# A reordered mixer, tail and merge in a single-core fp32 decoder layer

## The chip, the core and the metric

The kernel runs on one core of a Trainium2 chip: TensorE (PE) multiplies, VectorE (DVE), ScalarE (ACT) and GpSimd (POOL) do the elementwise work, SyncE (SP) and ScalarE issue transfers. The metric is the device time of one launch in microseconds; less is better.

## The reference

One layer of a hybrid decoder runs over 1024 prompt tokens and 8 × 8 sample tokens, width 1024, all in float32:

```python
x = x + 0.5 * swiglu(rmsnorm(x, g_ffn1), w1_gate, w1_up, w1_down)      # d_ff 2816
z = rmsnorm(x, g_mix) @ w_in       # mLSTM q,k,v,i,f,o | attention q,k,v (3 groups) | 2 gates
y_m = mlstm_scan(...) -> per-head rmsnorm, o-gate, @ w_up_m             # 4 heads, dk = dv = 128
y_a = dilated attention, (window, dilation) = (128,1), (512,4), (2048,16); groups combined
      by softmax denominators, @ w_up_a                                 # 4 heads of 64 a group
x = x + (sigmoid(gm) * y_m + sigmoid(ga) * y_a) @ w_out
x = x + 0.5 * swiglu(rmsnorm(x, g_ffn2), w2_gate, w2_up, w2_down)
y = rmsnorm(x, g_final)            # and the new states and caches
```

The sample tokens attend to cached keys and values of past tokens, eight sequences of eight tokens.

## The kernel before

Tokens stand in the free dimension, 1088 of them, in four quarters of 272. Each weight and each activation is split into a high part (rounded for the fast matmul format) and a low part; a product is three matmuls: high·high, high·low, low·high. Weights come in 99 slabs of 2048 columns by SyncE.

**Half steps.** The gate and up products use a scheme with seven products in place of eight (`WINO`, L85), a block of the weight slab and of the tokens each. For each, `fast` (L1036) waits for the low weight piece (`wcl_done`), for the token piece (`xprep`) and for free banks (`wino_step`, nine steps of VectorE a unit in `gate_part`). A unit is one slab and half of the tokens. GpSimd makes the low pieces (`low`, L843) and the sums of weight blocks (`less`, L850) of a slab in `gate_split`; ScalarE makes the high pieces: `PLAIN` ones from the slab itself, `SUMS` and `LAST` ones from the sums (L1522). Token pieces are made by `prepare` (VectorE, L2089 and L2095) and `token_high` (ScalarE, L1513). The first units of both half steps are written out one by one; a loop (two units per slab) follows. A unit of gates ends with a hidden row set stored by SyncE, and the down products read these rows back: `load_hidden` on the queue of `x_reload`, 22 times, with `accumulate` (L2132) adding into the residual.

**Mixer.** Queries, keys, values and gates are projected, then a program of 36 steps `w` (four heads, nine chunks) runs mLSTM chunk work, with one prompt attention unit of 35 (`UNITS`) beside each, `LEAD` = 3 units ahead. `att_exps`, `att_copy` run on ScalarE, `att_max`, `att_out` (L2471, L2472) on VectorE; SyncE stores each unit's rows (`store_outputs`) to `o_att`. The SP queue also loads caches and states in this stretch, in an order written out by hand.

**Tail.** After the steps come the last states, the last head's norm and turn (`turn_head`), then the sample attention in two quads of four sequences (`s_scores`, `s_max`, `s_exps`, `s_turn`, `s_values`, `s_out_turn`), with four groups of prompt rows loaded from `o_att` (`load_groups`), weighted and summed (`combine`, L2575 to L2592), transposed (`c_turn`, L1394) and stored (`store_pair`). GpSimd splits the three slabs of the up projection.

**Merge and out projection.** 32 units (quarter × eighth of the width) multiply the six branch pieces by the up slabs in two bank pairs; VectorE applies the gates from `sgate` (L2639, L2641, L2643), ScalarE makes the high part (L1954) and VectorE the low part (L2645) ahead of the next unit. `branch_high` and `branch_low` (L1912, L2607) split the next quarter's six branch pieces. GpSimd splits the first out-projection slab after the last unit (L829, L834). Then the out projection runs, with the norms and first slab of the second half step beside its end.

## Time and profile before

| | us |
|---|---|
| median of 3 runs | 2762.98 (2760.33 to 2774.57) |
| the profiled execution | 2771.38 |
| its span | 2769.5 |
| TensorE busy in it | 2514.5 |

One stretch follows another: start of the first half step to 112, its loop to 536, down products to about 840, projections to 1443, attention units ahead and mixer steps to 1657, tail to 1745.5, merge to 1850.5, a gap to 1861, out projection to 1960, start of the second half step to 2059.5, its loop to 2466, down products to 2740, last norm. To read the profile: a timeline row gives the start, the length and, in brackets, how long the engine sat idle before and what ended this; TensorE's granted clock is given as a share of its upper level of 2.4 GHz.

### The profile page before, as it was taken

The page shows a single profiled execution, that of the slowest core. Times are in us where ns is not written, and L with a number is a line of the kernel's source. Part 1 is how long each engine was busy: PE and PEld are TensorE (multiplying, and loading weights), DVE is VectorE, ACT ScalarE, POOL GpSimd, SP SyncE. Part 2 cuts the span into 40 slices and gives each one's busy share as a digit, 9 for nine tenths or more (in the row PEclk, how much of TensorE's full clock was granted, in tenths as well). Part 3 has the DMA queues.
Part 4 walks back from the last instruction along what each step waited for, and adds up shares of the span by engine and source line. Part 5 has one row for each costly group of instructions (what it writes and reads, how often), then busy time and mean ns, then how long its engine had stood idle before and what let it go on. Part 6 is the DMA issues. An engine that isn't in the chain of part 4 may idle for free. (4 is left out here: it accounts for less than half of the span.)

```text
span 2769.5 us, 47348 instructions
## 1 busy us (share of the span) xinstructions
PE 2514.5 (91%) x17550; PEld 2452.1 (89%) x17550; DVE 1261.0 (46%) x2482; ACT 593.7 (21%) x1165; POOL 1348.7 (49%) x1945
## 2 busy tenths in 40 slices
PE   4899999899999999999988885579789999989996
PEld 3899999899989999999986672579789999989996
DVE  6444434466684101332005555543653334446667
ACT  4322233110131011000114431111422323211012
POOL 5577777464445343444402313023557777746430
PEclk9899999999999999999997897789889999999998
DMA  2111221342213322222215737441112211143201
GB/s 113 70 70 74 78 81 70 144 164 94 78 35 127 127 96 92 88 93 98 78 53 173 231 122 287 159 137 64 67 51 74 89 70 74 70 189 131 94 16 65
DMA packets 112121, 282.89 MB, mean 102 GB/s; under 512 B 12996, under 2 KB 65404, under 8 KB 97020
## 3 DMA queue, kind: packets, MB, share of 16 engines
q1 hardware_dynamic: 87368, 251.65, 25.8%
q10 hardware_dynamic: 24628, 29.50, 3.0%
q8 instruction: 88, 1.44, 0.2%
q14 instruction: 37, 0.30, 0.0%
HBM read 206.25 MB, written 74.85 MB: 102 GB/s over the span
## 5 line engine op out<-in xcount | busy, mean ns | idle before, releaser
L1054 PE MATMUL ps<-chi,wch 128*128 128x272 f32 x2464 | 718.9, 292 | 50.7 <-POOL wcl L843 34.0
L1056 PE MATMUL ps<-chi,wcl 128*128 128x272 f32 x2464 | 717.5, 291 | 0.0
L829 POOL TENSOR_TENSOR wsp<-raw,con 128x256 fp32r<-128x256 f32 x440 | 269.8, 648 | 772.2 <-PE ps L979 284.8
L843 POOL TENSOR_TENSOR wcl<-raw,wch 128x256 fp32r<-128x256 f32 x616 | 450.7, 764 | 350.1 <-ACT wch L1522 350.1
L1054 PEld LDWEIGHTS ps<-chi,wch 128*128 128x128 f32 x2464 | 471.2, 191 | 53.7 <-POOL wcl L843 36.0
L1056 PEld LDWEIGHTS ps<-chi,wcl 128*128 128x128 f32 x2464 | 470.4, 191 | 0.0
L1055 PE MATMUL ps<-xlo,wch 128*128 128x272 f32 x1408 | 411.1, 292 | 0.0
L979 PE MATMUL ps<-act_hi,wsp 128*128 128x384 f32 (+1 forms) x1056 | 353.2, 334 | 23.6 <-DVE x L2132 14.8
L982 PE MATMUL ps<-act_lo,wsp 128*128 128x384 f32 (+1 forms) x1056 | 350.0, 331 | 0.0
L983 PE MATMUL ps<-act_hi,wsp 128*128 128x384 f32 (+1 forms) x1056 | 349.7, 331 | 0.0
L2132 DVE SCALAR_TENSOR_TENSOR x<-ps,x 128x384 f32<-128x384 f32 (+1 forms) x528 | 276.0, 532 | 161.7 <-PE ps L983 144.9
L834 POOL TENSOR_TENSOR wsp<-raw,wsp 128x256 fp32r<-128x256 f32 x440 | 326.1, 776 | 0.0
L1006 PE MATMUL ps<-h_hi,wsp 128*128 128x384 f32 (+1 forms) x960 | 314.6, 328 | 2.9 <-issue 1.8
L1010 PE MATMUL ps<-h_hi,wsp 128*128 128x384 f32 (+1 forms) x960 | 314.2, 327 | 0.0
L1009 PE MATMUL ps<-h_lo,wsp 128*128 128x384 f32 (+1 forms) x960 | 314.1, 327 | 0.0
L1055 PE MATMUL ps<-clo,wch 128*128 128x272 f32 x1056 | 304.8, 289 | 0.0
L1055 PEld LDWEIGHTS ps<-xlo,wch 128*128 128x128 f32 x1408 | 272.4, 193 | 0.0
L850 POOL TENSOR_TENSOR raw<-raw 128x256 f32<-128x256 f32 x352 | 261.8, 776 | 0.0
L1522 ACT ACTIVATE wch<-raw 128x512 fp32r<-128x512 f32 x308 | 182.8, 625 | 237.3 <-POOL raw L850 237.3
L979 PEld LDWEIGHTS ps<-act_hi,wsp 128*128 128x128 f32 x1056 | 201.8, 191 | 27.1 <-DVE x L2132 16.8
L982 PEld LDWEIGHTS ps<-act_lo,wsp 128*128 128x128 f32 x1056 | 201.9, 191 | 0.9 <-issue 0.6
L983 PEld LDWEIGHTS ps<-act_hi,wsp 128*128 128x128 f32 x1056 | 201.9, 191 | 0.0
(263 smaller groups left out, 3956.3 us busy)
## 6 DMA issues: line engine op xcount, KB each, us to landing
raw<-stream SPq DMA_DIRECT2D x99, 1024.0 KB, 4.8
hidden_out<-gout SPq DMA_DIRECT2D x88, 272.0 KB, 2.0
hst<-hidden_out SPq DMA_DIRECT2D x22, 1088.0 KB, 5.1
vc<-vc_in SPq DMA_DIRECT2D x8, 1170.0 KB, 7.8
kc<-kc_in SPq DMA_DIRECT2D x8, 1152.0 KB, 9.1
sgate<-zgate SPq DMA_DIRECT2D x32, 272.0 KB, 2.9
x<-xT SPq DMA_DIRECT2D x3, 2176.0 KB, 8.4
zgate<-stage ACTq DMA_DIRECT2D x16, 384.0 KB, 2.5
```

The costliest lines, as they stand in the source:

```text
L834: low_part = pool.tensor_tensor(wlo[j][:, cut], raw[:, j, cut], whi[j][:, cut].bitcast(F32), ALU.subtract)
L843: ins = pool.tensor_tensor(wcl[b][p][:, cut], raw[:, b, col + a:col + a + SPLIT], wch[b][p][:, cut].bitcast(F32), ALU.subtract)
L979: mm = pe.matmul(out, w_hi, x_hi, start=(k == 0), stop=False)
L982: pe.matmul(out, w_hi, x_lo, start=False, stop=False)
L983: last = pe.matmul(out, w_lo, x_hi, start=False, stop=(k == nk - 1))
L1006: mm = pe.matmul(out, w_hi, h_hi[:, k, a:a + w], start=(k == 0), stop=False)
L1009: pe.matmul(out, w_hi, h_lo[:, k, a:a + w], start=False, stop=False)
L1010: mm = pe.matmul(out, w_lo, h_hi[:, k, a:a + w], start=False, stop=(k == KT - 1))
L1054: pe.matmul(out, wch[b][p][:, cut], chi[q][p][:, k, :], start=(k == 0), stop=False)
L1055: pe.matmul(out, wch[b][p][:, cut], lo[:, k, :], start=False, stop=False)
L1056: mm = pe.matmul(out, wcl[b][p][:, cut], chi[q][p][:, k, :], start=False, stop=(k == 3))
L2132: dve.scalar_tensor_tensor(x[:, d, a:a + w], bank(4 + v % 4, w), 0.5, x[:, d, a:a + w], ALU.mult, ALU.add).then_inc(acc_free, 1)
```

## The change

- The order of the seven products, and with it that of the low pieces, the high pieces, the token pieces and the gate's steps, is another: the first two need plain pieces only. ScalarE's copy of a unit's first product waits for all nine steps of the unit before (it waited for seven). ScalarE makes sums and last pieces of the first slabs earlier. `load_hidden` goes ahead of `x_reload`, and VectorE waits for the second half of the reloaded residual only at the second group.
- Six attention units run ahead (`LEAD`), with head 0's first work at the fourth; stores go by ScalarE's queue.
- Quad 0 of the sample attention runs inside steps 29 to 35: query copies, scores, maxima, exponentials and turns; group 0 is combined there. Quad 1's values come inside the merge. Caches, group 0 and up slabs are asked for in the steps, each group's load and store by ScalarE's queue; ScalarE makes the up slabs' high parts.
- The merge has three bank pairs instead of two, and the low part of a unit comes one unit later; the kept residual is loaded at unit 16 instead of unit 2; the first out-projection slab is split in the last quarter into a place of its own (`out_hi`, `out_lo`).

The core of the diff:

```diff
-WINO = ((0, 9, 1), (1, 16, 6), (2, 17, 4), (3, 18, 5), (0, 14, 3), (1, 19, 2), (2, 10, 7))
+WINO = ((0, 9, 1), (1, 10, 2), (2, 16, 5), (3, 17, 4), (0, 18, 6), (1, 19, 3), (2, 11, 7))
...
+def next_branches(c, d):
+
+    if c == 0:
+        return (2 * d - 10, 2 * d - 9) if d >= 5 else ()
+    return (d - 2,) if d >= 2 else ()
+
+
+def out_bank(v):
+
+    return 4 + (v - AU_OUT + 2) % 4
...
-LEAD = 3
+LEAD = 6
+HEAD_AT = 3
+W_QUERY, W_SCORE, W_MAX, W_TURN, W_TURNED = 29, 31, 32, 33, 34
...
+                load_hidden(n, 0)
                 x_reload(n, 0)
-                load_hidden(n, 0)
...
+            def load_third():
+
+                sp.wait_ge(o_ready, last_of[0] + 1)
+                load_keys(2)
+                load_values(2)
...
+            for load in behind:
+                load()
...
                     else:
+                        sp.wait_ge(o_ready, last_of[1] + 1)
                         load_new(sqs, qr)
+                        for j in range(4):
+                            sp.dma_start(smk[SROW * j:SROW * j + SROW, :], amasks[0:SROW, A_SAMP:A_N]).then_inc(s_const, 16)
+                        load_new(sks, kr_out)
                         for b in (1, 2):
                             load_values_s(b)
...
+                if w + LEAD == last_of[0]:
+                    load_third()
...
+                    if h == H - 1:
+                        for s in range(2):
+                            sp.wait_ge(o_stored[s], 16 * len(UNITS[s::2]))
+                        sp.wait_ge(sqb_ready, 1)
+                        for n in range(2):
+                            sp.dma_start(oc[:, n], o_att[n * P:(n + 1) * P]).then_inc(c_in, 16)
+                        for i in range(3):
+                            slab(S_UP + i, (S_UP + i) % 3)
...
+                        load_vnw()
                         load_values_s(3)
...
+                        sp.wait_ge(sample_scored, 1)
+                        for b in range(4, 8):
+                            load_keys_s(b)
...
+            sp.wait_ge(sv_full, 1)
+            for b in (5, 6, 7):
+                load_values_s(b)
...
             sp.wait_ge(sample_scored, 2)
-            for i in (1, 2):
-                slab_behind(S_UP + i, (S_UP + i) % 3)
-            store_pair(1)
+            load_values_s(4)
...
+                    if c + 1 < NP:
+                        for k in next_branches(c, d):
+                            if k == 4 and c < 2:
+                                sp.wait_ge(mix_stored, 16 * (c + 3))
+                            load_branch(c + 1, k)
+                    if n == 10:
+                        sp.wait_ge(soT_ready, QUADS)
+                        for h in range(H):
+                            sp.dma_start(mix[4 + h // 2, 64 * (h % 2):64 * (h % 2) + 64, SEQ:TOK],
+                                         soT[:, h].rearrange("d b t -> d (b t)")).then_inc(hidden_stored, 16)
+                        sp.wait_ge(hidden_stored, 16 * 2 * H)
...
+                    if n == 16:
+
+                        sp.wait_ge(mix_stored, 16 * PAIRS)
                         sp.dma_start(x[:, 0:XB], x_kept[:, 0:XB]).then_inc(x_in[1], 16)
...
                 low(0, 0, 1)
-                low(5, 1536, 2)
-                low(4, 512, 3)
+                low(1, 512, 2)
+                low(5, 1536, 3)
                 less(0, 1024, 0)
                 less(1024, 1536, 1024)
                 pool.wait_ge(wsum_done, 4 * s + 1)
                 less(1536, 1536, 0)
-                low(2, 0, 4)
-                low(3, 1024, 5)
-                low(1, 1536, 6)
+                low(3, 0, 4)
+                low(2, 1536, 6)
+                low(4, 1024, 5)
                 pool.wait_ge(wsum_done, 4 * s + 3)
                 less(512, 512, 1536)
                 low(6, 512, 7)
...
+            for s in range(S_UP, S_UP + 3):
+                j = s % 3
+                for n, a in enumerate(range(0, SLAB, SPLIT)):
+                    cut = slice(a, a + SPLIT)
+                    pool.wait_ge(hi_split, s * PIECES + n + 1 - PIECES)
+                    low_part = pool.tensor_tensor(wlo[j][:, cut], raw[:, j, cut], whi[j][:, cut].bitcast(F32), ALU.subtract)
...
+            pool.wait_ge(up_full, PU_UP + 3 * KT)
+            pool.wait_ge(mx_ready, 6 * NP)
+            split(S_OUT, S_OUT // 3, S_OUT % 3, out_hi, out_lo)
...
-                    if p == 0 and not (isinstance(u, int) and u < 2):
-                        pe.wait_ge(wino_step, 9 * u - 10)
+                    if p < 3 and not (isinstance(u, int) and u < 2):
+                        pe.wait_ge(wino_step, 9 * u - (13, 12, 10)[p])
...
                 att_turn(u)
                 att_scores(u + 1)
-                if u == 0:
+                if u == HEAD_AT:
...
+                if w == W_SCORE:
+                    s_scores(0)
+                if w == W_TURN:
+                    s_turn(0)
             last_states()
+            s_values(0)
             for c in range(NC):
                 turn_head(H - 1, c)
...
+            s_out_turn(0)
             c_turn(0)
-            s_turn(0)
             s_scores(1)
-            s_values(0)
             c_turn(1)
             s_turn(1)
-            s_out_turn(0)
             c_turn(2)
-            s_values(1)
-            s_out_turn(1)
             c_turn(3)
...
+                    par = (KT * c + d) % 3
+                    pe.wait_ge(pair_free, unit)
...
+                    if (c, d) == (0, 1):
+                        s_values(1)
+                    if (c, d) == (0, 4):
+                        s_out_turn(1)
...
-            PLAIN = ((0, 0, 0), (5, 1536, 0), (4, 512, 0))
-            SUMS = ((2, 0, 1), (3, 1024, 2), (1, 1536, 3))
+            PLAIN = ((0, 0, 0), (1, 512, 0), (5, 1536, 0))
+            SUMS = ((3, 0, 1), (4, 1024, 2), (2, 1536, 3))
...
                 if half == 0:
                     act.wait_ge(wino_full, 7 * u + 1)
                     if not (isinstance(u, int) and u == 0):
-                        act.wait_ge(wino_step, 9 * u - 2)
+                        act.wait_ge(wino_step, 9 * u)
                     act.activation(gsil[:, 0, :], bank(4 * par, QW), ACT.Copy).then_inc(gate_silu, 1)
                 elif half == 1:
-                    act.wait_ge(wino_step, 9 * u + 5)
-                    act.activation(gsil[:, 0, :], gsil[:, 0, :], ACT.Silu).then_inc(gate_silu, 1)
+                    act.wait_ge(wino_step, 9 * u + 1)
+                    act.activation(gsil[:, 1, :], gsil[:, 1, :], ACT.Silu).then_inc(gate_silu, 1)
                 else:
                     act.wait_ge(wino_step, 9 * u + 8)
-                    act.activation(gsil[:, 1, :], gsil[:, 1, :], ACT.Silu).then_inc(gate_silu, 1)
+                    act.activation(gsil[:, 0, :], gsil[:, 0, :], ACT.Silu).then_inc(gate_silu, 1)
...
-                    token_high(0, 0)
                     act.wait_ge(x_in[2], 16)
                     half_square(1, 0)
                     half_square(1, 1)
+                    first_slab(0, SUMS)
+                    half_square(1, 2)
+                    half_square(1, 3)
+                    half_square(1, 4)
+                    token_high(0, 0)
                     token_high(0, 1)
                     token_high(0, 2)
-                    half_square(1, 2)
-                    half_square(1, 3)
+                    first_slab(0, LAST)
+                    gate_high(X + 1, b1, loaded + 16, PLAIN)
+                    half_square(1, 5)
                     token_high(0, 3)
                     token_high(0, 4)
...
+                    gate_silus(U, 0, 0)
+                    half_root(f1)
+                else:
+                    half_root(f1)
+                    gate_silus(U, 0, 0)
+                    first_slab(n, LAST)
+                    gate_high(X + 1, b1, loaded + 16, PLAIN)
+                gate_high(X + 1, b1, loaded + 16, SUMS)
                 gate_silus(U, 0, 1)
-                token_high(f1, 0)
-                gate_high(X + 1, b1, loaded + 16, SUMS)
+                gate_high(X + 1, b1, loaded + 16, LAST)
                 gate_silus(U, 0, 2)
                 gate_silus(U + 1, 1, 0)
+                gate_silus(U + 1, 1, 1)
+                token_high(f1, 0)
...
+            def store_outputs(u):
+
+                g, blk, h0, nh, nk = UNITS[u]
+                act.wait_ge(o_ready, u + 1)
+                o = o_att[:, g, h0:h0 + nh, :]
...
+            def up_high(s):
+
+                j = s % 3
+                act.wait_ge(raw_in[j], 16 * (s // 3) + (16 if j else 0))
+                act.wait_ge(slab_free, s + 1)
+                act.wait_ge(sample_scored, 2)
+                act.wait_ge(sv_full, 1)
+                for a in range(0, SLAB, SLAB // 2):
+                    cut = slice(a, a + SLAB // 2)
+                    act.activation(whi[j][:, cut], raw[:, j, cut], ACT.Copy).then_inc(hi_split, PIECES // 2)
...
-                if u == 0:
+                if u > 0:
+                    store_outputs(u - 1)
+                if u == HEAD_AT:
...
+                if u <= NU:
+                    store_outputs(u - 1)
...
+                if w == W_MAX:
+                    s_exps(0)
+                if w == W_TURN:
+                    group_exps(0)
+                if w == W_TURNED:
+                    s_turned(0)
             head_squares(H - 1)
+            next_group(1)
             head_roots(H - 1)
-
...
-            s_exps(0)
+            store_pair(0)
             group_exps(1)
-            s_turned(0)
+            next_group(2)
             s_exps(1)
+            for i in range(3):
+                up_high(S_UP + i)
+            store_pair(1)
+            s_turned(1)
+            group_exps(2)
+            next_group(3)
+            store_pair(2)
             for k in range(4):
                 branch_high(0, k)
-            s_turned(1)
-            group_exps(2)
             group_exps(3)
+            store_pair(3)
             for k in (4, 5):
                 branch_high(0, k)
...
-                if c == 3 and r == 3:
+                if c == 3 and r == 1:
                     act.wait_ge(slab_ready, S_OUT + 4)
                     first_slab(1, PLAIN)
-                if c == 3 and r == 5:
+                if c == 3 and r == 4:
                     first_slab(1, SUMS)
...
-                if m == 6:
-                    dve.wait_ge(wino_step, 9 * u + 6)
-                if m == 7:
-                    dve.wait_ge(wino_step, 9 * u + 4)
+                if m in (6, 7, 8):
+                    dve.wait_ge(wino_step, 9 * u + (6, 5, 4)[m - 6])
                 if m in (6, 8):
                     dve.wait_ge(gate_silu, 3 * u + m // 2 - 1)
-                out, one, two = ((S, B, G1), (U4, C, S), (gup[:], E, U4), (S, E, S), (G1, A, G1),
-                                 (Y1, B, U4), (Y1, G1, Y1), (G2, C, S), (Y2, G2, gup[:]))[m]
+                out, one, two = ((G2, B, G1), (S, C, G1), (U4, E, S), (gup[:], A, U4), (S, A, S),
+                                 (Y1, B, U4), (Y1, G2, Y1), (G1, C, S), (Y2, G1, gup[:]))[m]
                 dve.tensor_tensor(out, one, two, ALU.mult if m in (6, 8) else ALU.add).then_inc(wino_step, 1)
...
-                def downs(i, j):
+                def downs(i, j, first=False):
                     for c in range(NC):
+                        if first and c == 1:
+                            dve.wait_ge(x_in[2], 32 * (n + 1))
                         for d in range(KT):
...
             for u in range(LEAD):
                 att_out(u)
                 if u + 2 <= LEAD:
                     att_max(u + 2)
+                if u == HEAD_AT - 1:
+                    args(0)
+                    sample_arg(0)
+                    dve.memset(qwb[:], 0.0)
+                    link(dve.memset(ssq[:], 1.0))
...
+                if w == W_QUERY:
                     sample_queries()
+                if w == W_MAX:
+                    s_max(0)
+                if w == W_TURN:
+                    group_max(0)
+                if w == W_TURNED:
+                    s_turned(0)
+                    group_weigh(0)
+                if w == 9 * H - 1:
+                    group_sum(0)
             for part, o in (((0, 1, 2), (3, 0)), ((3, 4, 5), (2, 0)), ((6, 7), (3, 0))):
                 sample_states(H - 1, part, o)
             head_sums(H - 1)
+            s_outputs(0)
...
+            s_out(0)
             c_out(0)
-            s_turned(0)
             combine(1)
             s_max(1)
-            s_outputs(0)
+            c_out(1)
+            s_turned(1)
+            combine(2)
+            c_out(2)
...
             combine(3)
             c_out(3)
             for k in (4, 5):
                 branch_low(0, k)
...
+                    if n > 0:
+                        merge_low(n - 1)
+                    if (c, d) == (0, 2):
+                        s_outputs(1)
+                    if (c, d) == (0, 4):
+                        s_out(1)
+                    if c + 1 < NP:
+                        for k in next_branches(c, d):
+                            branch_low(c + 1, k)
+            merge_low(KT * NP - 1)
```

## Rows read from the trace of the kernel before

**Rows 1.** The page, parts 1 (busy) and 6 (KB each, us to landing).

```profile
PE 2514.5 (91%) x17550; PEld 2452.1 (89%) x17550; DVE 1261.0 (46%) x2482; ACT 593.7 (21%) x1165; POOL 1348.7 (49%) x1945
...
hst<-hidden_out SPq DMA_DIRECT2D x22, 1088.0 KB, 5.1
```

**Rows 2.** By stretch: length, engines' busy time, granted clock, DMA share, GB/s.

```profile
0.00:112.00 112.00, 63.21 (x384) 57.80 (x384) 71.83 (x84) 45.34 (x67) 53.58 (x65) 0.89 0.24 89
...
1474.00:1657.00 183.00, 157.17 (x1052) 132.13 (x1053) 110.96 (x357) 78.93 (x192) 48.12 (x93) 0.86 0.52 168
1657.00:1745.50 88.50, 37.30 (x439) 21.90 (x438) 52.13 (x91) 11.31 (x24) 33.63 (x48) 0.71 0.62 228
1745.50:1850.50 105.00, 84.24 (x576) 82.32 (x576) 58.77 (x144) 18.05 (x49) 0.00 (x0) 0.88 0.54 169
```

**Rows 3.** TensorE's waits, whole span: releaser, total us, times, longest.

```profile
PE ps L1054 <- POOL wcl L843: 34.0, 5, 10.7
PE ps L1394 <- DVE yat L2592: 30.1, 3, 16.0
...
PE ps L1054 <- DVE xlo L2095: 12.5, 3, 6.9
...
PE ps L979 <- POOL wsp L834: 10.6, 2, 10.4
...
PE ps L1287 <- DVE ao L2472: 6.2, 2, 4.5
```

**Rows 4.** Timeline of TensorE, first half step (start, us, instruction, idle before).

```profile
67.91 0.60 PE L1054 MATMUL ps<-chi,wch 128*128 128x272 f32 x1 [10.66 <-POOL wcl L843]
```

**Rows 5.** Groups on GpSimd in the first 115 us (count, busy, mean ns).

```profile
L843 POOL TENSOR_TENSOR wcl<-raw,wch 128x256 fp32r<-128x256 f32 x41 | 35.9, 906 | 58.9 <-ACT wch L1522 58.9
```

**Rows 6.** Timeline of TensorE where the first half step turns to down products.

```profile
540.79 0.55 PE L979 MATMUL ps<-act_hi,wsp 128*128 128x384 f32 x1 [4.45 <-DVE act_lo L2138]
...
551.46 0.69 PE L979 MATMUL ps<-act_hi,wsp 128*128 128x384 f32 x1 [4.66 <-DVE x L2132]
```

**Rows 7.** Timeline of the SP queue there.

```profile
528.45 0.71 SPq L522 DMA_DIRECT2D hst<-hidden_out  x1
```

**Rows 8.** Timeline of VectorE and GpSimd, a slab within the loop.

```profile
183.13 4.42 POOL L850 TENSOR_TENSOR raw<-raw 128x256 f32<-128x256 f32 x6
...
186.05 0.91 DVE L2118 TENSOR_TENSOR gout<-gsil,gout 128x272 f32<-128x272 f32 x1
```

**Rows 9.** The same at the loop's end, and TensorE's wait behind it.

```profile
499.27 4.22 POOL L850 TENSOR_TENSOR raw<-raw 128x256 f32<-128x256 f32 x6
...
502.24 7.08 DVE L2118 TENSOR_TENSOR gout<-gsil,gout 128x272 f32<-128x272 f32 x1
...
510.48 0.39 PE L1054 MATMUL ps<-chi,wch 128*128 128x272 f32 x1 [1.40 <-ACT gsil L1541]
```

**Rows 10.** Timeline of TensorE in the mixer: attention values, mLSTM scores.

```profile
1466.95 1.97 PE L1287 MATMUL ps<-av,apt 128*128 128x65 f32 x8
...
1484.69 0.28 PE L1166 MATMUL ps<-con,kT 128*128 128x128 f32 x1
...
1488.02 0.28 PE L1166 MATMUL ps<-con,kT 128*128 128x128 f32 x1
```

**Rows 11.** Waits in the mixer (engine, line, releaser: total us, times, longest).

```profile
DVE ao L2471 <- DMA o_att<-ao: 20.1, 4, 8.1
```

**Rows 12.** Timeline of TensorE in the tail.

```profile
1742.72 1.12 PE L1394 MATMUL ps<-con,yat 128*128 128x128 f32 x4 [13.65 <-DVE yat L2592]
```

**Rows 13.** Timeline of VectorE in the tail.

```profile
1729.31 8.32 DVE L2575 TENSOR_TENSOR ocm<-oc 128x8 f32<-128x8 f32 x1
```

**Rows 14.** Groups in the tail, both quads, all four groups.

```profile
L1374 PE MATMUL ps<-vc,spt 128*32 128x260 f32 x144 | 12.4, 520 | 2.1 <-issue 2.1
```

**Rows 15.** Groups in the merge.

```profile
L979 PE MATMUL ps<-mx_hi,wsp 128*128 128x272 f32 x192 | 61.0, 318 | 22.3 <-DVE mh_lo L2645 11.9 <-DVE mx_lo L2607 10.4
```

**Rows 16.** Timeline of TensorE, start of the second half step.

```profile
1993.56 0.60 PE L1054 MATMUL ps<-chi,wch 128*128 128x272 f32 x1 [10.32 <-POOL wcl L843]
```

595 lines of the change are left out of this document (269 added, 326 removed).

## The prediction

> **What bounds the kernel now.** I read the page's first part, the same figures by stretch, the waits of TensorE, and then the timeline of each stretch where it waits. TensorE is busy for 2514.5 of 2769.5 us [rows 1], so about 255 us are idle, and nothing that leaves TensorE's work as it is can gain more than that, apart from the clock. The change takes no matmul of the large products away. By stretch [rows 2]: the start of the first half step idles 112.0 - 63.2 = 48.8 us, the mixer's steps 183.0 - 157.2 = 25.8, the tail 88.5 - 37.3 = 51.2, the merge 105.0 - 84.2 = 20.8. The out projection's first split adds 10.6 at most [rows 3], and the second half step starts with waits, one of 10.3 [rows 16]. The loops between these stretches keep TensorE full; there the change matters only by the second rival.
>
> The sums below are made against the profiled execution, 2771.4 us (its span of 2769.5 and 1.9 around it). The median of the runs shown is 2763.0, 8.4 less.
>
> **A. First units of the first half step.** The new product order asks for plain weight pieces in its first two products, where the old one asked in its second for the sixth low piece, which GpSimd makes after the sums. That wait was 10.66 us [rows 4]. Over the whole span, waits for low weight pieces (34.0 in 5) and for the token sums' low part (12.5 in 3) are 46.5 us [rows 3], nearly all of it at the two starts; here they are 10.7 + 4.9 + 3.4 = 18.9 us on the path, so 27.6 at the second. Not all of it goes: GpSimd makes the same pieces, 41 low pieces took 35.9 us, 0.91 each [rows 5], and those of the last products still have to come. I let eight pieces by 0.91 = 7.3 us return as waits of later products, and take 18.9 - 7.3, rounded to 11. Ends: all three short waits kept and two thirds of the long one gone, 6; nearly all gone, 15. The new order of ScalarE's copies adds no instruction; the cover is its idle time (45.3 busy of 112 [rows 2]).
>
> **B. Turn from gate to down products, first half step.** TensorE waits 4.45 and again 4.66 us [rows 6]. The hidden rows are asked for at 528.45 [rows 7], 0.6 behind a residual reload on the same queue; the change swaps the two and lets VectorE wait for the last part of the residual only ahead of the second group. The load of the hidden rows then runs first on its queue, and lands, by the 5.1 us that such a load takes in the median [rows 1], before the gates end at 536. Both waits go: 9.1 us, and the down products' first matmuls run a little earlier at a higher granted clock; I take 9.5, ends 7 (half of the second wait comes back, for the residual comes later now) and 10.5. **G. The same turn in the second half step** has the same two waits, so 9.5 again, ends 7 and 13 because it starts from the lower granted clock there.
>
> **C and D. Mixer and tail.** Six attention units instead of three run ahead of the mLSTM steps, so the first step starts later: a unit took 4.4 us at the lower clock (the values at 1466.95 [rows 10] began 4.4 after those of the unit before), three more cost 13 to 17. In return the last three attention units leave the steps: with attention a step takes 3.33 us (two score matmuls at 1484.69 and 1488.02 [rows 10]), and three steps without it are cheaper by about 2 each, 6 to 7 together. VectorE's waits for stored attention rows, 20.1 us in four [rows 11], come from stores that stand on the SP queue behind cache loads; the stores now go by ScalarE's queue and should not wait for these loads. TensorE shares only part of that wait; I take 14 back, between 10 and 18. A wait of 4.5 us early in the steps, where VectorE stood behind GpSimd [rows 3], goes too. Inside the last seven steps the sample attention of quad 0 is added: its query copies, scores, row maxima, exponentials and transposes. In the tail the same work took about 15 us of TensorE and VectorE time one after the other, so the steps get 14 to 17 longer. Sum: 15 - 6.5 - 14 - 4.5 + 15 = +5, the steps end at 1662 instead of 1657.
>
> The DMA issues move as well: 35 attention stores go from SP to ScalarE, 29 of them in the steps, at 0.4 to 0.7 us of issue each (0.71 for a larger one [rows 7]), which ScalarE has (78.9 of 183 busy [rows 2]). Behind each store wait on ScalarE's queue stand the next exponentials. The store of a unit is placed two exponentials behind its own work, so that it finds its rows written; if they are late, ScalarE stops, and TensorE with it. Bounds: nothing (a gain is excluded, the issue is only moved), and 29 by 0.4 = 12 us; I take nothing, since TensorE is what ends a step.
>
> Here the Trainium skill speaks against the move, "DMA: Bandwidth & Descriptors", section "Queues, rings and completion order": each DMA engine takes turns between the queue rows it has work for, by packets, so that a second queue escapes the order of the first but not its traffic. With DMA at 0.52 of its time in these steps [rows 2] I read it so that the stores go through at once but more slowly; by the rule taken alone half of the 14 us would stay, and the sum would be 7 us worse. Waits of up to 8.1 us [rows 11] look like a queue's order rather than a shared engine, so I stay with 14.
>
> The tail is the larger gain. From the end of the steps to the merge are 88.5 us, 51 of them idle on TensorE [rows 2], and 30.1 of these are waits for combined attention groups [rows 3]: the last came 13.65 us late [rows 12], behind a VectorE instruction that took 8.32 us [rows 13] while GpSimd split the up-projection weights. After the change the chain is, from the end of the steps: values of quad 0, half of 12.4 [rows 14] and the wait ahead, 11; turn of the heads to 16; group 0 combined meanwhile, its matmul at 19; group 1 at 24, one group being 5 us of small VectorE work; scores and maxima of quad 1; high parts of the up weights on ScalarE, six of about 1 us by an estimate; exponentials of quad 1 at 35; group 2, then the load of group 3, landing at about 44; group 3 and its transposes to 50; the last two branch parts stored and read back to 55. So 55 in place of 88.5, with ends 45 (group loads hidden) and 75 (each of two loads seen in full, 10 us each). Merge begins at 1662 + 55 = 1717 instead of 1745.5: gain 28.5, ends 10 and 40.
>
> **E. Merge and first out-projection split.** The merge's 84.2 busy us at a granted clock of 0.88 are 74 at full clock [rows 2]; of its idle time 22.3 us come from late low parts and quarter boundaries [rows 15]. Delaying the low part by one unit takes VectorE's part off the path, and the early split of the out weights takes off the wait of 10.4 that follows the merge [rows 3]. Added: values of quad 1 and their turn, 6.2 + 1.0 [rows 14]. New sum: 74 + 7 + three quarter boundaries of 2.6 + a clock start of 3 + 8 of DMA waits, since the residual's load of 3.3 MB and the store of sample rows still stand ahead of gate loads. That is 100 against 105.0 + 10.4 = 115.4: gain 15, ends 5 (values and one long gate wait stay on the path) and 28 (none does).
>
> **F. First units of the second half step.** The 27.6 us from above, 10.32 of them in one wait [rows 16]. The same reordering applies, and ScalarE starts the first slab one step earlier, but ScalarE's and GpSimd's work of a slab is the same, and the residual's norm still comes ahead. I take 40%, 11; ends 6 and 16.
>
> **Sum.** 11 + 9.5 + 9.5 + 28.5 + 15 + 11 = 84.5. 2771.4 - 84.5 = 2686.9 for a profiled execution, 8.4 less for the median: **2679 us**. The low ends add to 41 (2722), the high ones to 122.5 (2640).
>
> **Rivals.** First, **the tail does not shrink**: the group loads from memory and VectorE's chain set the merge's start, as they do now with waits of up to 16.0 us [rows 3], and the added work in the steps costs what the shorter tail saves. For it: one set of load buffers, now beside cache loads and up weights. Against: the first group and three up slabs are asked for inside the steps. Then C and D give 3 instead of 28.5, and E 8: 2763 - 52 = **2711**. Chance 0.12.
>
> Second, **VectorE is locked out in each slab of the loops**. At 186.05 the combination of two SBUF inputs took 0.91 us, 2.92 behind GpSimd's first subtraction at 183.13 [rows 8]; at 502.24, 2.97 behind it, it took 7.08 and ended only when GpSimd paused, and TensorE then waited 1.40 [rows 9]. The change rearranges both engines' order in a slab, and lets the next unit's ScalarE copies wait for the whole previous unit (two combinations more, about 0.6), so a blocked slab costs 1.4 + 0.6 = 2.0. If VectorE comes 0.05 us later against GpSimd in each of the 40 slabs, that is 80 us, and the gain is nearly gone: 2763 - 84.5 + 80 = **2759**. For it: the two rows are only 0.05 us apart. Against: the long form stands only three times in this trace, at the ends of the loops, and VectorE's work of a slab is not lengthened. Chance 0.08.
>
> Of this the Trainium skill says, in "SBUF — State Buffer", section "Who interferes with whom", that a VectorE instruction with two SBUF inputs and a GpSimd instruction that reads SBUF exclude each other, the first holding the shared ports for its whole instruction. The row agrees that it blocks; its 7.08 us are ten GpSimd instructions of 0.70, where the rule gives one. By the rule a meeting would cost 0.7 us, within what the loop takes without a wait, and this rival's time would be the forecast's.
>
> Third, **slower than before**: the same lock, from the same point, but in every place where the new order puts VectorE behind running GpSimd work. Besides the 80 us it then strikes the four first units, 2 us each, and the tail: the quad maxima and group combinations wait until GpSimd's 24 low parts of the up weights have ended, and the 8.32 us row [rows 13] becomes 10 more. 80 + 8 + 10 = 98 against 84.5, 2763 + 14 = **2777**. It decides from the point at which VectorE's combination comes more than 2.95 us after the first subtraction. Chance 0.06.
>
> **How the numbers follow.** Forecast 0.74, first rival 0.12, second 0.08, third 0.06. About 0.5% (14 us) is what a measurement of this kernel can tell from no change. Faster by over that: forecast and first rival, 0.86; within it: the second, 0.08 (2759); slower: 0.06. The range takes in the bounds of the sum, 2640 to 2722, and the first rival with some spread: 2643 to 2735.
>
> **What would show it.** A: the second product of the first pass follows its first without a gap. B: the hidden rows are asked for ahead of the residual, and neither of the two waits at the turn is over 1 us. C: no wait of VectorE for stored attention rows above 3 us; the steps end near 1662. D: 55 us from there to the merge's first matmul. E: no 10 us gap after the merge, 100 us for the stage. F: 11 us off the first units. In the loops the two-input combination stays at 0.9. The forecast fails where a slab of the loop shows 7 us in that row, or where the tail stays above 75 us because a group's load or a moved store is late.

## The result and the profile after

The changed kernel takes 2728.2 us in the median (2723.5 to 2732.6, four runs) against 2764.9 of the kernel before: ratio 0.986, interval 0.984 to 0.988. The forecast was 2679 in a range of 2643 to 2735: the time lies inside the range, near its slow end, and less than half of the expected 84.5 us came (37 us between the medians). The profiled execution has a span of 2727.0 us, 42.5 less than that of the kernel before, and its parts can be read stage by stage.

The page's first part, and the stretches that answer to [rows 1] and [rows 2] (start of the first half step, attention ahead with the first step, the other steps, tail, merge; columns as there):

```profile
PE 2500.2 (92%) x17548; PEld 2432.9 (89%) x17550; DVE 1249.4 (46%) x2482; ACT 599.1 (22%) x1171; POOL 1337.3 (49%) x1921
```

```profile
0.00:107.00 107.00, 63.51 (x375) 55.87 (x375) 73.28 (x83) 44.61 (x65) 54.03 (x60) 0.87 0.24 91
1434.00:1481.50 47.50, 23.02 (x122) 16.52 (x121) 15.55 (x40) 13.67 (x31) 8.51 (x17) 0.66 0.81 244
1481.50:1658.00 176.50, 148.61 (x1080) 122.40 (x1082) 108.38 (x356) 76.07 (x186) 38.72 (x77) 0.88 0.50 168
1658.00:1720.80 62.80, 28.74 (x268) 17.91 (x266) 43.11 (x80) 15.48 (x27) 20.15 (x24) 0.66 0.74 268
1720.80:1823.80 103.00, 86.75 (x664) 82.41 (x664) 58.42 (x145) 18.14 (x49) 10.22 (x16) 0.91 0.53 170
```

The last step ends only near 1664 here, so the fourth row still holds some 6 us of the steps.

TensorE's waits over the span, beside [rows 3]:

```profile
PE ps L982 <- DVE x L2195: 26.2, 8, 7.1
PE ps L1369 <- DVE yat L2614: 21.8, 2, 12.5
...
PE ps L1057 <- DVE xlo L2160: 20.0, 5, 9.5
...
PE ps L982 <- DVE mx_lo L2636: 13.2, 3, 6.4
PE ps L1291 <- DMA av<-va_out: 11.9, 1, 11.9
...
PE ps L1057 <- ACT gsil L1550: 9.6, 6, 5.6
...
PE ps L1209 <- DVE Cs L2475: 7.2, 1, 7.2
...
PE ps L982 <- DVE mh_lo L2710: 3.0, 1, 3.0
...
PE ps L1057 <- POOL wcl L836: 3.0, 3, 1.7
```

Four more rows of the same view of the kernel before:

```profile
PE ps L979 <- DVE x L2132: 15.5, 7, 4.7
...
PE ps L1166 <- DMA v<-vm: 10.6, 1, 10.6
...
PE ps L1054 <- ACT gsil L1541: 3.9, 3, 1.4
...
PE ps L1287 <- DMA av<-va_out: 2.1, 1, 2.1
```

The wait for low weight pieces, 34.0 us before, has nearly gone (3.0), and the merge's 10.6 us split too (0.2). In their place stand the token pieces (`xlo`, 20.0 against 12.5), the down accumulation (26.2 against 15.5), ScalarE's copies of the gates (`gsil`, 9.6 against 3.9) and, in the mixer, `Cs`. The wait of 11.9 us for the first attention values (`av`) is no new loss: the kernel before waited 10.6 us for `v` and 2.1 for `av` in that place.

Taking the same matmul in both timelines as a mark gives what each stage gained (us, before less after):

| stage | forecast | measured |
|---|---|---|
| A, start of the first half step | 11 | 3.2 |
| end of its loop | 0 | 1.7 |
| B, turn and down products | 9.5 | 3.6 |
| projections | 0 | 1.8 |
| C, attention ahead and steps | -5 | -16.4 |
| D, tail | 33.5 | 30.9 |
| E, merge, split, out projection | 15 | 14.0 |
| F, start of the second half step | 11 | 7.4 |
| end of its loop | 0 | 1.7 |
| G, turn and down products | 9.5 | -6.2 |
| last norm | 0 | 0.8 |
| sum | 84.5 | 42.5 |

Tail and merge came nearly as forecast, the second start with two thirds of its 11 us. Four terms did not come: A, B, C and G together are 41 us short, nearly the whole miss of 42. Each entry compares one profiled execution with another: the projections, which should not change, take 620.6 to 627.2 us in the profiles of kernels that leave GpSimd's splits as they are, so an entry can be off by a few us.

### The profile page after: what moved, and what is told of

The parts are those of the page before. It is cut to its first block and busy times, and to the rows that moved or that the text cites. A ratio compares the mean times of both kernels' runs of the same rounds, so it can differ in the third digit from the quotient of the medians.

```text
span 2727.0 us, 47602 instructions
## 1 busy us (share of the span) xinstructions
PE 2500.2 (92%) x17548; PEld 2432.9 (89%) x17550; DVE 1249.4 (46%) x2482; ACT 599.1 (22%) x1171; POOL 1337.3 (49%) x1921
## 5 line engine op out<-in xcount | busy, mean ns | idle before, releaser
L836 POOL TENSOR_TENSOR wcl<-raw,wch 128x256 fp32r<-128x256 f32 x616 | 457.6, 776 | 334.2 <-ACT wch L1531 334.2
L822 POOL TENSOR_TENSOR wsp<-raw,con 128x256 fp32r<-128x256 f32 x408 | 250.0, 648 | 602.3 <-PE ps L982 287.0
L827 POOL TENSOR_TENSOR wsp<-raw,wsp 128x256 fp32r<-128x256 f32 x408 | 301.2, 774 | 0.0
```

The costliest lines, as they stand in the source:

```text
L827: low_part = pool.tensor_tensor(lo[:, cut], raw[:, j, cut], hi[:, cut].bitcast(F32), ALU.subtract)
L836: ins = pool.tensor_tensor(wcl[b][p][:, cut], raw[:, b, col + a:col + a + SPLIT], wch[b][p][:, cut].bitcast(F32), ALU.subtract)
```

## What happened at the four places

**The turn.** After, around 531 to 552 us, SP, ScalarE, VectorE and TensorE:

```profile
533.65 0.55 SPq L528 DMA_DIRECT2D x<-xT  x1
...
535.00 0.43 SPq L535 DMA_DIRECT2D hst<-hidden_out  x1
...
548.73 0.84 ACT L1565 ACTIVATE act_hi<-hst 128x768 fp32r<-128x768 f32 x1 [14.70 <-DMA hst<-hidden_out]
549.60 1.37 DVE L2201 TENSOR_TENSOR act_lo<-hst,act_hi 128x768 fp32r<-128x768 f32 x1 [8.36 <-ACT act_hi L1565]
...
551.50 0.69 PE L982 MATMUL ps<-act_hi,wsp 128*128 128x384 f32 x1 [6.61 <-DVE x L2195]
```

The first wait of [rows 6] is gone, from 4.45 to 0.42. The second one has grown from 4.66 to 6.61 and ends at the same 551.5 us as before: VectorE stands in its order behind the low part of the next hidden rows, which land 13.7 us after they are asked for, behind the residual's second half and a weight slab on the queue.

The second turn has one more wait:

```profile
2444.82 4.61 POOL L822 TENSOR_TENSOR wsp<-raw,con 128x256 fp32r<-128x256 f32 x8
2447.59 8.11 DVE L2201 TENSOR_TENSOR act_lo<-hst,act_hi 128x768 fp32r<-128x768 f32 x1 [0.38 <-ACT act_hi L1565]
...
2449.39 5.50 POOL L827 TENSOR_TENSOR wsp<-raw,wsp 128x256 fp32r<-128x256 f32 x8
...
2456.16 0.63 PE L982 MATMUL ps<-act_hi,wsp 128*128 128x320 f32 x1 [6.03 <-DVE x L2195]
```

The low part took 8.11 us where its median is 0.96. It ends at 2455.7, 0.8 us after the GpSimd run (2454.9) whose last 16 instructions stand above. I call a VectorE row that ends only behind such a run a long row, and the effect the lock. It is the lock of the second rival, but on another instruction than I named.

**The mixer.** Waits between 1500 and 1545 us, after:

```profile
DVE Cp L2467 <- DMA c_out<-Cp: 9.8, 1, 9.8
...
PE ps L1209 <- DVE Cs L2475: 7.2, 1, 7.2
```

SP's order there:

```profile
1516.86 0.32 SPq L604 DMA_DIRECT2D aqk<-qr  x1
...
1521.16 1.60 SPq L689 DMA_DIRECT2D c_out<-Cp  x1
```

SP issued eight key loads and one value load of the third group first, from 1516.86 on, and head 0's state store only at 1521.16, behind them. VectorE waits for that store before it may overwrite the state. In the kernel before the store came first.

**The first start.** The third unit's third product is the late one now, in place of the second unit's second ([rows 4]):

```profile
86.19 0.57 PE L1057 MATMUL ps<-chi,wch 128*128 128x272 f32 x1 [9.30 <-DVE xlo L2160]
```

## The experiments

My theory after the two traces: each missing gain was returned at the next wait (A, B), the state store (C) and the lock (G). Rivals stand with the runs. Ratios are to the kernel before, with their intervals. Where a run's whole time hides a stage, the stage is read from its timeline, that is, from one execution.

**The two halves apart.** The parts of the diff for the half steps alone, and all the rest alone.

> The kernel before with the half steps' part of the change alone (product order, order of pieces and of ScalarE's copies, hidden rows ahead of the residual). Theory, the half steps' gains were given back at the next wait: read from the two traces they are 3 + 2 at the first start and the end of its loop, 4 at its turn, 7 + 2 at the second start, and a loss of 6 at the second turn, so about 11 us under the kernel before (ratio 0.996). Had my four terms held, 41 us (0.985). Rival, the two halves of the change disturb one another: then this kernel alone comes near 41.

> The kernel before with mixer, tail, merge and first out-projection split of the change alone. Theory: 14 us from mixer and tail and 14 from merge and out projection, together 28 under the kernel before (ratio 0.990). By my terms it would be 43.5 (0.984). If the halves disturb one another, this gives clearly more than 28, and the two kernels' gains do not add to that of the whole change.

Half steps alone: 0.997 (0.994 to 0.9998). The rest alone: 0.992 (0.990 to 0.995), 21 us. The halves add up to 29 against 39 of the whole change, with intervals that touch; no gain of the size I had forecast is hidden in either. The half steps gave 8 us of 41: the largest part of the miss is there.

**The swap undone.**

```diff
-                load_hidden(n, 0)
                 x_reload(n, 0)
+                load_hidden(n, 0)
...
+                dve.wait_ge(x_in[2], 32 * (n + 1))
-                downs(0, (S_D[n] + 1) % 3, True)
+                downs(0, (S_D[n] + 1) % 3)
```

> The changed kernel with the residual's reload again ahead of the hidden rows, and VectorE's wait for the whole residual again ahead of the first group, in both half steps. My terms B and G say that this costs 19 us against the changed kernel. Theory, the turn is set by the transfers that can start only after the last gates, so that what the first wait gives the second takes: at most 5 us are lost in the first half step, the second TensorE wait falls from 6.6 to 4 or 5 there, and in the second half step the 8.1 us row of VectorE's activation low part may go, so between 4 us faster and 6 us slower than the changed kernel.

0.988 (0.983 to 0.994): by the ratios 7 us slower than the changed kernel, with intervals that overlap. TensorE's first wait is back (4.72 us at the first turn, 5.91 at the second), and its second is 4.93 and 4.36. From the start of the last gate matmul to the end of the last down product it took 288.4 and 282.8 us, the changed kernel 282.0 and 289.6, the kernel before 285.7 and 283.4. So the swap saved no 19 us. The first figure includes a low part of 4.63 us; the second has none, and there the swapped order without a long row, below, takes 278. The swap is worth some 5 us there, where I wrote 9.5.

**The third group's loads later.**

```diff
-                if w + LEAD == last_of[0]:
+                if w + LEAD == last_of[0] + 2:
                     load_third()
```

> The changed kernel with the loads of the third group's keys and values issued two steps later, so that head 0's state store stands ahead of them on the SP queue. Theory: VectorE's 9.8 us wait for that store, and TensorE's wait of 7.2 us behind it, go, 4 to 8 us faster than the changed kernel. Rival, the transfer engines are full in this stretch whatever the order: the wait moves to the next load, and the time stays within 2 us.

0.982 (0.979 to 0.985), 11 us less than the changed kernel by the ratios, 8 between the medians. The store is issued ahead of the loads, and both waits shown for the mixer are gone:

```profile
1514.04 0.34 SPq L689 DMA_DIRECT2D c_out<-Cp  x1
```

The steps 1 to 12 take 48.2 us where the changed kernel took 59.2 and the kernel before 56.0; over all profiles with six units ahead they take 48.2 to 48.7 with the later loads and 58.9 to 61.4 without. The whole of stage C takes 209.5 us in place of 224.5 (208.0 in the kernel before). So the cause of C's loss is shown. This run also had no long row at the second turn, 278.0 us. Its gain over the changed kernel has therefore two causes.

**The low part one group later**, from here on with the third group's loads later.

```diff
-                        hidden_low(i + 1, c, j)
+                        if not first:
+                            hidden_low(i + 1, c, j)
+                        elif c > 0:
+                            hidden_low(i + 1, c - 1, j)
+                    if first:
+                        hidden_low(i + 1, NC - 1, j)
```

> The kernel with the third group's loads two steps later, and in the first round of down products VectorE's low part of the next hidden rows one group later in its order. Theory: TensorE's second wait at the turn (6.6 us in the first half step, 7.1 in the second) is VectorE standing behind the next hidden rows, which are loaded behind the residual's second half and a weight slab; the down products do not need that low part yet. Then the second wait falls to 2 us or less and each turn gains 4 to 5. Rival: VectorE stands behind the residual's second half itself; the waits stay within 1 us of 6.6, no gain.

0.976 (0.973 to 0.980). TensorE's second wait is 0.65 us at the first turn and 0.71 at the second, in place of 6.6 and 5.4 with the later loads alone. The stretch takes 279.9 us at the first, in spite of a low part of 5.12 us later in it, and 271.7 at the second, 6.4 less. TensorE's next wait at the first turn, then VectorE's rows at the place of the old one:

```profile
564.77 0.44 PE L982 MATMUL ps<-act_hi,wsp 128*128 128x384 f32 x1 [0.65 <-DVE x L2195]
```

```profile
548.64 0.56 DVE L2195 SCALAR_TENSOR_TENSOR x<-ps,x 128x384 f32<-128x384 f32 x1 [0.50 <-PE ps L986]
551.15 1.49 DVE L2195 SCALAR_TENSOR_TENSOR x<-ps,x 128x384 f32<-128x384 f32 x3 [1.95 <-DMA x<-xT]
```

The residual is 1.95 us late here, and TensorE does not feel it. The second wait was VectorE's order, not the residual.

**Pauses in GpSimd's splits.**

```diff
+                    if n:
+                        pool.wait_ge(low_split, s * (PIECES - 1) + n - (PIECES - 1))
                     low_part = pool.tensor_tensor(lo[:, cut], ...)
+                    if n + 1 < PIECES:
+                        low_part.then_inc(low_split, 1)
```

(and the same with `hi_split` for the high parts.)

> The kernel with the third group's loads two steps later, and each GpSimd instruction of a slab's split waiting for the one before it to end. Theory of the lock: a VectorE instruction with two SBUF inputs that meets running GpSimd work gets in only when GpSimd pauses; with a pause after each instruction no low part of hidden rows takes over 2 us beside a split, where it took 8.11 us once in the changed kernel and 4.63 to 8.35 in two other runs. The gate's combination beside the other GpSimd routine is left as it is and may still show 7 us. Time within 3 us of the kernel with later loads, 6 us less where that one had a long row in the down products. Rival: what frees VectorE is the end of GpSimd's work, and the long rows stay.

> The changed kernel with each GpSimd instruction of a slab's split waiting for the one before it to end, and nothing else. Theory: the 8.11 us row of VectorE's activation low part in the second half step goes, and with it some 10 us of the second turn and its down products (289.6 us from the last gate to the last down product in the changed kernel, 278 to 280 here). The whole is 5 to 10 us faster than the changed kernel. Rival: the second turn's loss is the transfers', and it stays above 285 us.

Whole times: 0.977 (0.975 to 0.980) on top of the later loads, by the ratios 13 us less than with these alone, which is more than I had expected and not explained; and 0.984 (0.981 to 0.988) on the changed kernel alone, a median of 2728.4 us against 2728.2, by the ratios 5 us less and well inside the intervals. The lock is gone from the low parts of hidden rows: in the four profiles with paused splits none of 264 takes over 1.6 us, in the ten others 30 of 660 take over 2. Changed kernel, then the changed kernel with pauses (count; shortest, median and longest in ns):

```profile
L2201 DVE TENSOR_TENSOR act_lo<-hst,act_hi x66: 818/959/8110, 530.9 to 2676.8; 128x768 fp32r<-128x768 f32 x44, 128x640 fp32r<-128x640 f32 x22
```

```profile
L2210 DVE TENSOR_TENSOR act_lo<-hst,act_hi x66: 818/958/1541, 532.3 to 2674.5; 128x768 fp32r<-128x768 f32 x44, 128x640 fp32r<-128x640 f32 x22
```

The second turn takes 277.9 us in place of 289.6, as the theory said; the later loads without a pause also had 278.0 there, so the count of long rows is the stronger evidence. The 5 to 10 us for the whole are neither shown nor excluded. The profiled execution lost 4.4 us in the projections and had two 7 us rows in the gate loops, where nothing was changed (2.6 and 2.4 us of delay).

**Four units ahead.** `LEAD` 4 and `HEAD_AT` 1 in place of 6 and 3.

> The kernel with the third group's loads two steps later, and four attention units ahead of the steps in place of six. In the traces a unit ahead costs 4.0 to 4.4 us (lower clock, one unit after the other), a unit inside a step 1.6 to 2. Theory: the first step starts 8 to 9 us earlier, the steps are 3 to 4 us longer, so 4 to 6 us faster. My term C (13 to 17 us for three units, 6.5 back) says 5 us. Rival: the units in steps 29 and 30 meet the sample attention there and the gain is lost by the end of the steps.

0.983 (0.978 to 0.988), no gain in the whole, for this profile holds two long low parts (9.07 and 8.12 us) and turns of 292.1 and 288.7. In the mixer, from the first attention matmul to the second step's scores 36.2 us in place of 47.5, and from there to the last step 168.3 in place of 161.9: 4.9 us gained, within the expected 4 to 6, though each side was mis-sized by 2 to 3.

**The second half's reciprocal earlier.** `half_root` of the second half ahead of the first unit's copy, `half_inverse` ahead of its combinations.

> The kernel with the third group's loads two steps later, and the reciprocal of the second half's norm, first half step, made on VectorE ahead of the first unit's combinations instead of behind five of them. Theory: what replaced the waits for low weight pieces at the first start is the chain of token pieces on VectorE, so moving 3.5 us of it ahead takes 3 to 4 us off the 9.3 us wait of TensorE at the third unit, and the loop starts 3 to 4 us earlier. Rival: the third unit is held by GpSimd's or ScalarE's pieces, and the wait stays.

0.981 (0.978 to 0.985). The loop starts 3.7 us earlier (sixth unit), as expected. The 9.3 us row itself stays, because the products ahead of it moved as well:

```profile
82.84 0.57 PE L1057 MATMUL ps<-chi,wch 128*128 128x272 f32 x1 [9.08 <-DVE xlo L2160]
```

The token chain of VectorE sets the first start. The whole shows no gain over the later loads: a low part of 8.41 us stands in the first turn (292.1 us).

**Together.** All five edits in one, then with pauses in the gate slabs' routine too.

> Third group's loads two steps later, low part of the next hidden rows one group later in the first down round, reciprocal of the second half's norm ahead of the first combinations, four attention units ahead in place of six, pauses in the splits. If the parts add: against the kernel with later loads alone, 4 to 5 and 6 at the two turns, 4 at the start, 5 in the mixer: 18 to 20 us less, 2690 to 2705, ratio to the kernel before 0.973 to 0.976. Rival: what one part gives the next wait takes, and it is no faster than the best of them alone (0.976 to 0.977).

> The same with pauses between GpSimd's instructions in the gate slabs' routine too. Theory of the lock: no two-input combination of the gates takes over 2 us in the loops any more, which saves 2 to 8 us (two to four rows of 7 us in each profile, each with 1.4 to 4 us of TensorE behind it). Rival: the pauses lengthen a slab's 16 us of GpSimd to about 18, and the first units, which wait for it, lose 2 to 4 us each.

All five: 2702.1 us, 0.974 (0.972 to 0.977), the fastest median of the study and within what was expected, though its interval overlaps that of the later low part (0.973 to 0.980), so the rival is not excluded. At the turns TensorE now waits 4.2 and 3.7 us for GpSimd's paused splits (279.3 and 274.9 us), and the projections took 633.1 us against 625.0 to 625.4 in the other three profiles with paused splits, which no run explains. All six: 0.978 (0.976 to 0.981), 10 us more than all five between the medians. The two-input combination of the gates in the two, all five first:

```profile
L2190 DVE TENSOR_TENSOR gout<-gsil,gout x88: 435/510/7232, 60.4 to 2406.0; 128x272 f32<-128x272 f32 x88
```

```profile
L2213 DVE TENSOR_TENSOR gout<-gsil,gout x88: 441/713/999, 60.0 to 2412.4; 128x272 f32<-128x272 f32 x88
```

No gate row is over 1 us any more. But from the fifth to the seventh unit the first start takes 29.5 us in place of 24.6 and the second 28.0 in place of 24.7: the rival's price, 3 to 5 us each, is more than the long rows had cost (in all five a wait of 1.7 us behind each of two).

**The changed kernel again.**

> The changed kernel once more, nothing altered. If the long rows of the lock depend on where VectorE and GpSimd happen to stand (their distance differs by hundredths of a microsecond between a row of 0.9 and one of 7), this profile has them at other places than the first one: no 8 us row at the second turn, that turn at 278 to 280 us from the last gate to the last down product in place of 289.6, and perhaps another row elsewhere. If they are fixed by the program's order, the row of 8.1 us and the 289.6 us come again within 1 us.

0.985 (0.978 to 0.991), its profile 17.1 us longer than the first one. The parts differ like this: a gate row of 7.45 us at 139.8 delays the first loop by 4.2 us, a low part of 8.59 us the first turn by 10.2 (292.2), the projections take 4.2 us more, and the second turn (a low part of 8.77, the turn's fifth, as in the first profile) takes 286.4 instead of 289.6. The low part of the first turn, and GpSimd's run beside it:

```profile
562.35 8.59 DVE L2201 TENSOR_TENSOR act_lo<-hst,act_hi 128x768 fp32r<-128x768 f32 x1 [0.38 <-ACT act_hi L1565]
```

```profile
560.04 4.63 POOL L822 TENSOR_TENSOR wsp<-raw,con 128x256 fp32r<-128x256 f32 x8
564.62 5.51 POOL L827 TENSOR_TENSOR wsp<-raw,wsp 128x256 fp32r<-128x256 f32 x8
```

So the program does not fix how often the lock strikes. The place at a turn it does: all seven low parts over 8 us in the profiles are the fifth of their turn, and a long row came again at the second turn. The expectation that it comes again within 1 us falls, and so does the one that it does not come. Over all profiles with the swapped order and VectorE's old order, a turn without a low part over 8 us takes 282.0 to 282.7 us at the first and 277.5 to 278.7 at the second, one with such a row 292.1 to 292.2, and 286.4 to 289.6. Such a row in the down products costs 8 to 12 us.

Most meetings of the two engines pass. In the first profile of the changed kernel 39 of the 66 low parts overlap a running GpSimd instruction, and three of them take over 2 us; of the 88 gate combinations 45 do, and none is long. What decides between the two is not shown.

## Why the prediction was wrong

**B and G.** The failed step is "Both waits go". The swap took the first wait as I said. For the second I had written half a return as the worst end, and named the residual; the row that ends it is the low part of the next hidden rows in VectorE's order. Moving that one instruction group gives the rest: 271.7 us at the second turn against 283.4 in the kernel before, 11.8, more than my 9.5. G's sign came from the lock: 289.6 with it, 278 without. I had the lock as a rival, priced as a 2.0 us delay in each of 40 slabs, on the gate's combination and, in the third rival, at the first units and in the tail; I had put it at nothing in the down products. It strikes a few times in an execution, at several kinds of VectorE instruction, and costs up to 12 us there.

**C.** The failed step is the sum "15 - 6.5 - 14 - 4.5 + 15". Its terms by stretches: attention ahead 17.8 longer (15 forecast), steps 1 to 12 longer by 3.2 (4.5 shorter forecast), steps 13 to 27 shorter by 11.1 (14), the rest longer by 6.7 (8.5). The store of attention rows on ScalarE's queue did most of what I took: VectorE's waits for these rows fell from 20.1 [rows 11] to 4.1, though they are back at 8.3 to 12.9 in the runs with the later loads and six units ahead.

```profile
DVE ao L2534 <- DMA o_att<-ao: 4.1, 2, 3.7
```

What I did not follow is the queue they left: with the stores gone, `load_third` moved ahead of head 0's state store on SP, and VectorE waited 9.8 us. I had looked at what stands behind the moved instruction, and not at what it had held back.

**A.** Two steps failed. "I let eight pieces by 0.91 = 7.3 us return" named GpSimd's pieces; low weight pieces hardly wait now, but VectorE's chain of token pieces makes TensorE wait 9.3 us. And "the cover is its idle time" put ScalarE's new order at nothing: the first product comes at 48.34 in place of 43.98. From that product to the eighth unit the start is 7.6 us shorter, and 4.4 of these are lost ahead of it. The half steps' part brings the delay: with it alone the first product comes at 47.46, with the rest alone at 44.82. Read from ScalarE's timeline, the last two squares for the second half's norm now stand behind copies of token pieces that wait for VectorE; no run moves them alone.

**D, E and F** came near: 30.9 of 33.5, 14.0 of 15, 7.4 of 11. In the tail the last two groups still wait 9.2 and 12.5 us for VectorE's combination; that the chain is shorter because quad 0 and group 0 are done in the steps is read from the order, and no run takes the parts from one another. E's sum is near by luck in part. The split's wait went as forecast, from 10.4 to 0.3, and the late low part too (`mh_lo`, 11.9 [rows 15] to 3.0), but the quarter boundaries cost 13.2 us (`mx_lo`), not three times 2.6. So the merge itself is only 1.9 us shorter, and the out projection behind it gave 2.0 that I had not put in. The terms of 3 us for the clock and 8 for DMA waits are not shown by any run. At the second start TensorE still waits 9.5 us for token pieces, and 5.6 for a copy of ScalarE's that stands behind a long row of a third kind:

```profile
1942.10 6.63 DVE L2149 SCALAR_TENSOR_TENSOR x<-x,con,fsum 128x544 f32<-128x544 f32 x1
```

Its shortest of 32 is 0.77 us. The three profiles with the gates' routine unpaused that have no such row there are about 1 us shorter at this start, so it is not the whole of what F lacks. The 1.7 us at the end of each loop is luck: the kernel before has a long gate row there, the changed kernel's first profile has none, and its second one loses 4.2 us to one in the first loop.

**The rivals.** The tail shrank, so the first is out. The second and third have the right mechanism in the wrong form. The 0.05 us point in the loop does not decide: 2.93 us behind the first subtraction the gate's row is short in the changed kernel and takes 7.15 us with the later loads.

Small slips in my working do not change this: 18.9 - 7.3 is 11.6, not 11; the second start's waits were 26.8 us, not 27.6; 1.7 of the merge's 22.3 us lie ahead of it; one of the three long gate rows before, at 2051.64, is at a loop's start; and the range's low end should be 2640.

What stays open: what decides whether a low part meets the lock; why the projections took 620.6 us in the first profile of the changed kernel and 623 to 627 in the others that leave GpSimd's splits as they are; and whether a long row in the down products stands in every execution of the changed kernel, for only two were profiled.

## What to carry to other kernels

When a transfer is pulled ahead, ask which instruction of the in-order consumer comes next and what it waits for: here one low part in VectorE's order cost as much as the reordered load had saved. When an instruction leaves a queue, read what moves up in that queue too. A two-input VectorE instruction beside a long GpSimd run is a risk to look for in every stage. A pause between GpSimd's instructions removed the long rows here, but it makes GpSimd's work longer, which cost more than it gave where other engines wait for that work.

## What the runs showed of the hardware

A VectorE instruction with two SBUF inputs that meets GpSimd's back-to-back run mostly passes, but some last until the run ends. Such rows took 2.6 to 9.1 us in the down products, where the median is 0.96, and 6.7 to 7.5 in the gate combinations. Over all profiles, each low part over 2 us ended 0.8 us after GpSimd's run and each such gate combination 0.3 us after it. Waiting after each GpSimd instruction (0.10 us more for each) brings the longest to 1.4 to 1.5 us for the low parts and to 1.0 for the gates. The Trainium skill, "SBUF — State Buffer", section "Who interferes with whom", says that the one that holds the shared ports blocks the other for its whole instruction. The long rows agree that VectorE is blocked; one GpSimd instruction there is 0.58 to 0.70 us, so in the rows over 7 us VectorE is kept out by ten or more in a row, where I had read the rule as one.
